# Prompt attention of a hybrid decoder step: turned probabilities round three banks, one bank for both groups' value sums, first turn ahead of the last tile's values

## The reference

```python
p_s = masked_softmax(s_s.reshape(B, Q, G, R, -1), m_s).reshape(s_s.shape)
o_s = jnp.einsum('bqgrnk,bgqnkd->bqgrd', p_s, vs.astype(f32))
s_w = jnp.einsum('bqgrd,bwgd->bqgrw', qg, kw.astype(f32))
p_w = masked_softmax(s_w, m_w[None, :, None, None, :])
o_w = jnp.einsum('bqgrw,bwgd->bqgrd', p_w, vw.astype(f32))
o = g[..., 0:1] * o_c + g[..., 1:2] * o_s + g[..., 2:3] * o_w
```

## Time and profile before

| | us |
|---|---|
| median of 3 runs | 1165.59 (1165.34 to 1168.35) |
| the profiled execution | 1165.77 |
| its span, first to last instruction | 1164.0 |
| TensorE matmuls busy | 1097.6 (94%) |
| TensorE weight loads busy | 860.3 (74%) |
| VectorE busy | 686.2 (59%) |
| ScalarE busy | 333.0 (29%) |
| GpSimd busy | 307.1 (26%) |
| the 32 tiles, from the first turn to the last value matmul | 281.4 to 361.3 |

### The profile page before, as it was taken

The page is one execution under the profiler, slowest core; times in us unless marked ns, Lnnn a source line. Parts: engine busy times, 40 slices in busy tenths (PEclk is TensorE's granted clock), DMA queues, the critical chain, the costliest instruction groups (busy, mean ns, idle before and its releaser), DMA issues.

```text
span 1164.0 us, 19165 instructions
## 1 busy us (share of the span) xinstructions
PE 1097.6 (94%) x7598; PEld 860.3 (74%) x7598; DVE 686.2 (59%) x1463; ACT 333.0 (29%) x785; POOL 307.1 (26%) x346
## 2 busy tenths in 40 slices
PE   7899999878999799999998998999999999999995
PEld 5677777654557577788886876888878888778884
DVE  4743332688887687788884356454465444654235
ACT  2111110625774355445453023211111111000005
POOL 7300000164648677767841011000020000000000
PEclk9899999877999999999999998999999999999998
DMA  9733331145404666777645113221122212321102
GB/s 354 284 148 148 149 147 56 49 191 143 126 2 160 254 272 257 290 308 306 273 183 200 37 73 145 86 95 73 72 79 101 72 72 74 126 100 40 60 1 77
DMA packets 36839, 165.30 MB, mean 142 GB/s; under 512 B 4968, under 2 KB 15816, under 8 KB 27608
## 3 DMA queue, kind: packets, MB, share of 16 engines
q1 hardware_dynamic: 25304, 94.78, 22.3%
q0 software_dynamic: 11312, 69.38, 15.5%
q10 hardware_dynamic: 144, 0.04, 0.0%
HBM read 158.84 MB, written 9.24 MB: 144 GB/s over the span
## 4 chain that ended last, share of the span: by engine, by line
PE 83%; DVE 8%; ACT 4%; POOL 2%; DMA 2%; issue 1%; ACTq 0%; DVEq 0%; POOLq 0%
PE PS L366 80%; PE PS L1147 1%; ACT ringreg L1660 1%; PE PS L1193 1%; ACT trunk L1847 1%; DMA ringreg<-in_w_ada_dram 1%; POOL zreg L671 1%; DVE w L2422 1%; DMA sreg<-in_cmp_dram,idxc 1%; POOL sreg L650 1%; DVE sreg L2208 1%; DVE sreg L2108 0%; DVE creg L2108 0%; ACT sreg L1527 0%; DVE ringreg L2187 0%
## 5 line engine op out<-in xcount | busy, mean ns | idle before, releaser
L366 PE MATMUL PS<-mixreg,w 128*128 128x272 f32 (+1 forms) x596 | 139.8, 387 | 9.9 <-DVE mixreg L2103 4.2
L366 PE MATMUL PS<-creg,ringreg 128*128 128x272 f32 (+1 forms) x564 | 144.4, 400 | 3.6 <-ACT creg L1535 2.9
L366 PEld LDWEIGHTS PS<-mixreg,w 128*128 128x128 f32 x596 | 110.7, 196 | 31.9 <-issue 8.3
L366 PEld LDWEIGHTS PS<-creg,ringreg 128*128 128x128 f32 (+1 forms) x564 | 104.7, 188 | 33.3 <-issue 10.1
L366 PE MATMUL PS<-zreg 128*32 128x128 f32 (+4 forms) x832 | 107.3, 327 | 2.4 <-ACT ringreg L1647 2.0
L366 PE MATMUL PS<-creg,w 128*128 128x256 f32 (+1 forms) x432 | 104.8, 388 | 0.0
L366 PE MATMUL PS<-mixreg,ringreg 128*128 128x272 f32 (+1 forms) x404 | 100.4, 400 | 1.0 <-DVE sreg L2440 1.0
L366 PEld LDWEIGHTS PS<-creg,w 128*128 128x128 f32 x432 | 81.0, 191 | 14.7 <-issue 2.3
L366 PEld LDWEIGHTS PS<-mixreg,ringreg 128*128 128x128 f32 (+1 forms) x404 | 75.2, 189 | 17.8 <-DVE sreg L2440 1.5
L366 PE MATMUL PS<-mixreg,sreg 128*128 128x272 f32 x352 | 87.2, 395 | 0.0
L366 PEld LDWEIGHTS PS<-zreg 128*32 128x32 f32 (+2 forms) x832 | 72.9, 143 | 18.3 <-issue 7.8
(11 more groups left out here) (394 smaller groups left out, 1936.4 us busy)
## 6 DMA issues: line engine op xcount, KB each, us to landing
ringreg<-in_w_ada_dram SPq DMA_DIRECT2D x24, 1024.0 KB, 7.3
ringreg<-in_w_f_dram SPq DMA_DIRECT2D x22, 1024.0 KB, 4.8
ringreg<-in_w_in_dram SPq DMA_DIRECT2D x11, 1024.0 KB, 4.9
ringreg<-in_w_f_dram SPq DMA_DIRECT2D x8, 704.0 KB, 4.3
creg<-in_w_f_dram SPq DMA_DIRECT2D x8, 704.0 KB, 6.7
sreg<-in_win_dram SPq DMA_DIRECT2D x8, 512.0 KB
out_dram<-in_win_dram SPq DMA_DIRECT2D x1, 4064.0 KB
trunk<-in_x_t_dram SPq DMA_DIRECT2D x4, 544.0 KB, 5.4
```

Of the source, the lines that this page charges most:

```text
L366: return nc.tensor.matmul(o, lhsT, rhs, start=start, stop=stop, **kw)
```

## The change

On TensorE, `turned` is split into its halves. For each t the queue becomes `scores(t + 2)`, first half of `turned(t)`, `values(t - 1)`, second half of `turned(t)`. The halves go in turn into banks 6, 7 and 5, in place of 6 and 7 alone. Bank 5 is freed by putting both groups' value sums into bank 4, side by side; `values(t)` therefore waits for the output of tile t - 1 in place of t - 2. ScalarE and VectorE keep their order and read from the new places. Tile 1 has an extra wait for the GLA work that used bank 5.

```diff
+        def turn_bank(t, q):
+
+            return (6, 7, 5)[(2 * t + q) % 3]
...
-            def turned(t):
+            def turned(t, q):
                 j, pb = t // 2 % TT, PB[t % 3]
-                for q in range(2):
-                    pe.wait_ge(sem("nsa_p"), 2 * t + q + 1)
-                    for k in range(j + 1):
-                        last = nc.tensor.transpose(PS[:, 6 + q, k * P:(k + 1) * P], pb[:, q * LP + k * P:q * LP + (k + 1) * P], ident[:, :])
-                    last.then_inc(sem("nsa_pt"), 1)
+                if t == 1:
+                    pe.wait_ge(sem("gla_done"), GH)
+                pe.wait_ge(sem("nsa_p"), 2 * t + q + 1)
+                for k in range(j + 1):
+                    last = nc.tensor.transpose(PS[:, turn_bank(t, q), k * P:(k + 1) * P], pb[:, q * LP + k * P:q * LP + (k + 1) * P], ident[:, :])
+                last.then_inc(sem("nsa_pt"), 1)
...
-                if t >= 2:
-                    pe.wait_ge(sem("nsa_out"), t)
-                elif t == 0:
+                if t >= 1:
+                    pe.wait_ge(sem("nsa_out"), t + 1)
+                else:
                     pe.wait_ge(sem("gla_done"), GH + 1)
...
-                        last = matmul(PS[rows, 4 + g, 0:P], VT[:, k, c + g * HD:c + (g + 1) * HD], pt[:, (4 * q + k) * P:(4 * q + k + 1) * P],
+                        last = matmul(PS[rows, 4, g * P:(g + 1) * P], VT[:, k, c + g * HD:c + (g + 1) * HD], pt[:, (4 * q + k) * P:(4 * q + k + 1) * P],
...
+                turned(t, 0)
                 if t >= 1:
                     values(t - 1)
-                turned(t)
+                turned(t, 1)
             values(NTL - 1)
```

More of the change, by code:

```diff
@@ L1659, in _ @@
                     act.wait_ge(sem("nsa_pt"), 2 * t + 1 + q)
-                    nc.scalar.activation(pt[:, 4 * q * P:4 * q * P + w], PS[:, 6 + q, 0:w], ACT.Copy).then_inc(sem("nsa_ptev"), 1)
+                    nc.scalar.activation(pt[:, 4 * q * P:4 * q * P + w], PS[:, turn_bank(t, q), 0:w], ACT.Copy).then_inc(sem("nsa_ptev"), 1)
             def exponential(b, q, c0, w):
@@ L2199, in output @@
                 o = MIXT[g * HD:(g + 1) * HD, 4 + t // 8, j * P:(j + 1) * P]
-                link(nc.vector.tensor_tensor(o, o, PS[g * HD:(g + 1) * HD, 4 + g, 0:P], ALU.add))
-                nc.vector.tensor_tensor(o, o, PS[HD - g * HD:P - g * HD, 4 + g, 0:P], ALU.add).then_inc(sem("nsa_out"), 1)
+                link(nc.vector.tensor_tensor(o, o, PS[g * HD:(g + 1) * HD, 4, g * P:(g + 1) * P], ALU.add))
+                nc.vector.tensor_tensor(o, o, PS[HD - g * HD:P - g * HD, 4, g * P:(g + 1) * P], ALU.add).then_inc(sem("nsa_out"), 1)
             def turn_in(b, k):
```

## The result

| us | before | after |
|---|---|---|
| median of 9 runs | 1166.84 (1165.34 to 1168.66) | 1173.55 (1168.47 to 1174.28) |
| the profiled execution | 1165.77 | 1171.97 |
| its span | 1164.0 | 1170.2 |
| loop, first turn to last value matmul | 281.37 to 361.31: 79.94 | 283.35 to 368.39: 85.04 |
| behind the loop | 802.7 | 801.8 |

The ratio is 1.0049, with an interval of 1.0034 to 1.0064: some 6 us slower. Forecast were 1169.0 and at most 1171.2. So the stage is compared by its own length, and that has grown by 5.1 us.

A forecast was written before the change was run, and what follows sets the result against it. TensorE was taken as close to the limit, VectorE next. Group changes +4.6, eviction waits -3.6, GpSimd waits +2.7 and a wait before scores -0.3 gave +3.4 us: 1169.0, range 1166.4 to 1171.2.

The forecast's parts named there:

- A change of kind costs 0.15 us, so a tile of four groups costs more: TensorE, tiles 1 to 29: one added group change per tile, 1.24 us per eight-tile period, 4.6 us over the stage.
- Eviction waits go, waits for GpSimd take their place: TensorE in the loop: waits on ScalarE's evictions fall by 3.6 us, waits for GpSimd's scaling grow by 2.7 us.
- the layout: Four engine queues laid out in written order with durations from the profile; gave +3.4 us for the new order.
- Rivals 1 and 2: 1: added mode change is free, 1167.0, chance 0.20. 2: evictions are the limit, nothing replaces them, 1162.1, chance 0.09.
- Banks free no one, the stricter wait costs nothing in the new order: Third half bank frees no engine; values waiting for the output of t-2 behind a first half cost nothing.
- Rival 4: Stricter wait binds if VectorE falls behind: 0.2 us in four narrow tiles of eight, +3 us, 1172; chance 0.07.
- The loss is passed on whole by GpSimd and the gather: Loop's end: last scaling moves by 3.35 us, TensorE's end by 3.4, and all behind it moves by that.
- First stretch +1.4 us: Loop up to the scores of tile 10: own work +1.2, eviction waits -0.6, GpSimd waits +0.8.
- Rival 3: Clock rises later because the second tile's first half waits some 0.4 us for GpSimd; 1.7 us more, 1170.7; chance 0.12.
- Its +0.4 there: Last stretch of the loop: own work +0.9, eviction waits -1.5, GpSimd waits +1.1, a further -0.1.

The follow-up runs named there:

- added_change: Kernel before plus one identity turn into empty bank 7 behind the first of each tile's value matmuls: 1179.99 us, ratio 1.0108.
- order_alone: Changed kernel's new order, but with the two half banks, two accumulator banks and loose output wait of before: 1168.65 us, ratio 1.0022.
- w_banks: Kernel before with 16 + 6 extra identity turns, three half banks, one accumulator bank and the stricter wait, in old order: 1161.13 us, ratio 0.9953.
- new_from2: Changed kernel with the old order in tiles 0 and 1 alone, new order from tile 2 on: 1171.89 us, ratio 1.0035.
- warm2_before: Kernel before plus 16 identity turns behind the scores of tile 1 and 6 ahead of the turn of tile 1: 1161.33 us, ratio 0.9954.
- warm_before: Kernel before plus 16 identity turns into an unread bank behind the scores of tile 1: 1161.81 us, ratio 0.9950.

## Why the prediction was wrong, point by point

- **A change of kind costs 0.15 us, so a tile of four groups costs more: right.** The row at 342.31 and the bare turn of `added_change` show it.
- **Eviction waits go, waits for GpSimd take their place: right**, nearly in size too. Worked out from the starts of all groups in the third stretch, TensorE's own work grew by 1.23 us (1.24 forecast), waits on evictions fell by 0.9 (0.75) and those for GpSimd grew by 0.5 (0.39). The middle and last stretches came out to within 0.15 us of the layout, in every kernel with the new order. Rivals 1 and 2 (19.4 and under 18.7 us) fall with them.
- **Banks free no one, the stricter wait costs nothing in the new order: right**, to 0.14 us a period (`order_alone`). Rival 4 did not happen. With the old order the wait would have cost: 6.8 us of waits and 1.5 us of loop in `w_banks`.
- **The loss is passed on whole by GpSimd and the gather: right** (89.1 for 83.8 us).
- **First stretch +1.4 us: wrong, and this is the step that failed.** The layout took the clock's rise 9 us after the first turn from the earlier trace rows as if the change could not move it. It came at 10.9 to 15.1 us in the five traces with the new order, and the first stretches there are 22.67 to 24.47 (mean 23.6) against 20.41 and 20.24: +3.3, not +1.4. In the two traces of the changed kernel itself it is +2.8, and that makes the loop's +4.7 (84.56, mean of two, against 79.85) where +3.4 was forecast.
- **Rival 3 had the effect, but the wrong cause and price.** It hung the late rise on one wait, which `new_from2` took away without result, priced a rise 2.8 us later at 1.7 us, though half clock can lose at most half of such a stretch, 1.4, and got 0.12 because no row said whether that wait mattered. What no row decides should have had a larger share. The right question was what the new order does to TensorE in all the tiles at half clock; the range ended at 1171.2 for want of it.
- **The rest.** Loop +4.7, median +5.5 to +6.7: 1 to 2 us have no place in the traces. The two traced executions of after (1171.97 and 1168.54 us) were 1.6 and 4.6 us faster than the medians beside them, those of before (1165.77 and 1168.84) lay within 1.1 us of theirs, so the traces may show a late rise as shorter than it mostly is; that is not shown. The same holds with the clock held up (loop +2.1 and +2.3, median +3.1 and +5.25, layout +2.8). Medians of the kernel before scatter by about 1 us: the forecast set out from 1165.6, and the nine runs beside the changed kernel gave 1166.84, which is 1.25 us of the 2.35 by which the range was missed.
- **One reading.** The forecast has no other engine reach TensorE's share. In the last stretch VectorE is busier (18.69 us for 18.49). Its +0.4 there came out all the same.

Which property of the new order keeps the clock down is not settled. For "more and shorter groups": `added_change` and `new_from2` rise late, with no wait of TensorE from the first turn to the rise. That it is the order in tiles 2 to 7 is shown, by one or two traces of each kernel; so is that extra turns in TensorE's gaps hold the clock up.

## What to carry over

Where a stretch runs at half clock, its end is not a constant of the kernel: treat "when does the clock come up" as an unknown of its own, bounded by a rise several us later, whenever a change alters what TensorE does before that point. A reorder that trades waits on one engine for waits on another should be summed with the price of every added group, by starts in the timeline: here each was small, and right. Idle time just ahead of a stage that starts at half clock is worth a look, but at its true price: 22 turns that compute nothing made the traced loop of the kernel before 0.9 us shorter and that of the changed kernel 3.4. The medians moved by 5 to 9 us, some 4 us of it by a gap 260 us further on that had gone with the edit. A median alone would have put that down to the clock: compare the whole of two traces, not the changed stage only.

## What the runs showed of the chip

- **A few instructions more can take away a gap elsewhere.** With the 22 extra turns the kernel before is at 1160.10 us, 0.9942 [0.9924, 0.9961]. Only 0.9 us of that is in the traced loop (79.07 for 79.94). Behind the loop it is 798.0 us in place of 802.7 (797.6 in `warm2_before`, 801.2 in `warm_before`), and 4.0 of these 4.7 us lie in the one place where TensorE stood still before, 260 us behind the loop's end. `order_alone`, without any extra turn, lacks the gap as well (796.4).
- **The same program meets the lower clock at other places in each execution.** Behind unchanged code the first turn lies at 281.37 and 285.06 in the two traces of before.
- **Values of the two halves run beside each other.** They write different partitions of a bank. Two matmul records of one half alone take 0.21 us beyond the change, four of both halves 0.22. The Trainium skill, "TensorEngine Tiling (Array Packing)", section Key Properties, says that different tiles can run their weight loads and matmuls in parallel; the rows of `added_change` agree, and cutting between such a pair costs 0.21 us on top of the changes of kind.
